# Latent attention in a two-block stack: scores from one 128-row product per head, and a new order of filler tiles

## The reference

```python
u = rms_norm(h, mix_norm[l])
c_q, c_kv, k_pe, hq, hf, hi, hg, ga, gb = split_cols(u @ w_in[l], IN_SPLITS)
y_a = mla(c_q, c_kv, k_pe, pos, q_norm[l], kv_norm[l], w_uq[l], w_ukv[l]) @ w_proj_attn[l]
y_b = hgrn2(hq, hf, hi, hg, lbs[l], hg_norm[l]) @ w_proj_rec[l]
merged = jax.nn.sigmoid(ga) * y_a + jax.nn.sigmoid(gb) * y_b
h = h + merged @ w_out[l]
# in mla: 8 heads, 64 plain + 32 rotated features
q = jnp.concatenate([q[..., :QK_NOPE], rope(q[..., QK_NOPE:], pos)], axis=-1)
k = jnp.concatenate([kv[..., :QK_NOPE], jnp.broadcast_to(k_rot, (B, L, H, QK_ROPE))], axis=-1)
s = jnp.einsum('bqhd,bkhd->bhqk', qi, k).astype(jnp.float32) * scale   # then causal softmax, times v
# rope: [x1*cos - x2*sin, x2*cos + x1*sin]
```

## Time and profile before

| | |
|---|---|
| median of 3 runs | 2515.24 us (2514.94 to 2517.25) |
| the profiled execution's own time | 2509.26 us |
| its span | 2507.3 us |
| TensorE matmul busy | 2368.4 us, 94% |
| DVE, ACT, POOL busy | 56%, 47%, 22% |
| mean granted TensorE clock over the span | 0.964 of full |
| DMA | 380 MB, mean 152 GB/s |
| chain that ended last | TensorE 64%, issue 27%, DVE 3%, POOL 2%, ACT 1% |

### The profile page before, as it was taken

The page is one execution under the profiler, slowest core; times in us unless marked ns, Lnnn a source line. Parts: engine busy times, 40 slices in busy tenths (PEclk is TensorE's granted clock), DMA queues, the critical chain, the costliest instruction groups (busy, mean ns, idle before and its releaser), DMA issues.

```text
span 2507.3 us, 50416 instructions
## 1 busy us (share of the span) xinstructions
PE 2368.4 (94%) x18374; PEld 2294.9 (92%) x18374; DVE 1412.1 (56%) x1968; ACT 1178.1 (47%) x1764; POOL 557.9 (22%) x589
## 2 busy tenths in 40 slices
PE   7999999999999999989999999986999999988998
PEld 7999886799999999877899989986999999987998
DVE  6556753455545556744655555467654655464553
ACT  5445533344435436433454355456654445445552
POOL 4321000043213310000332133123432123111320
PEclk9999998899999999988999999998999999988999
DMA  5554222245545544221355445533455455532553
GB/s 208 178 186 154 99 95 90 95 156 186 177 159 172 197 142 144 92 77 68 128 181 183 165 141 194 192 122 113 156 196 197 147 195 191 195 124 69 196 197 109
DMA packets 99270, 380.31 MB, mean 152 GB/s; under 512 B 10911, under 2 KB 13087, under 8 KB 99144
## 3 DMA queue, kind: packets, MB, share of 16 engines
q1 hardware_dynamic: 99144, 378.63, 44.5%
HBM read 377.52 MB, written 3.16 MB: 152 GB/s over the span
## 4 chain that ended last, share of the span: by engine, by line
PE 64%; issue 27%; DVE 3%; POOL 2%; ACT 1%; POOLq 1%; DVEq 1%; DMA 0%; ACTq 0%; SPq 0%
PE bank L564 20%; PE bank L566 20%; PE bank L565 20%; PE bank L625 1%; PE bank L626 1%; PE bank L627 1%; POOL midlo L1964 1%; POOLq L1919 1%; ACT whi L962 0%; PE bank L582 0%; POOLq L1907 0%; DVE cv L1694 0%; DVE wlo L1356 0%; DVE xlo L1367 0%; POOL reclo L1959 0%
## 5 line engine op out<-in xcount | busy, mean ns | idle before, releaser
L1356 DVE TENSOR_TENSOR wlo<-raw,whi 128x1024 fp32r<-128x1024 f32 (+1 forms) x660 | 873.2, 1334 | 531.6 <-ACT whi L962 530.9
L564 PE MATMUL bank<-xhi,wlo 128*128 128x272 f32 (+1 forms) x3392 | 984.2, 290 | 4.4 <-DVE z L1710 3.9
L566 PE MATMUL bank<-xhi,whi 128*128 128x272 f32 (+1 forms) x3392 | 978.0, 288 | 0.0
L565 PE MATMUL bank<-xlo,whi 128*128 128x272 f32 (+1 forms) x3392 | 976.0, 288 | 0.0
L962 ACT ACTIVATE whi<-raw 128x1024 fp32r<-128x1024 f32 (+1 forms) x660 | 729.1, 1117 | 494.1 <-PE bank L566 466.1
L564 PEld LDWEIGHTS bank<-xhi,wlo 128*128 128x128 f32 x3392 | 649.8, 192 | 7.8 <-issue 5.8
L566 PEld LDWEIGHTS bank<-xhi,whi 128*128 128x128 f32 x3392 | 648.8, 191 | 0.0
L565 PEld LDWEIGHTS bank<-xlo,whi 128*128 128x128 f32 x3392 | 648.1, 191 | 0.0
L564 PE MATMUL bank<-hidhi,wlo 128*128 128x272 f32 (+1 forms) x1408 | 400.5, 284 | 0.0
L566 PE MATMUL bank<-hidhi,whi 128*128 128x272 f32 (+1 forms) x1408 | 399.5, 284 | 0.0
L565 PE MATMUL bank<-hidlo,whi 128*128 128x272 f32 (+1 forms) x1408 | 399.3, 284 | 0.0
(11 more groups left out here) (319 smaller groups left out, 2662.0 us busy)
## 6 DMA issues: line engine op xcount, KB each, us to landing
raw<-ffn_gu SPq DMA_DIRECT2D x352, 512.0 KB, 3.5
raw<-ffn_down SPq DMA_DIRECT2D x128, 704.0 KB, 4.1
raw<-mix SPq DMA_DIRECT2D x120, 512.0 KB, 3.5
raw<-rec SPq DMA_DIRECT2D x28, 512.0 KB, 3.7
raw<-kv SPq DMA_DIRECT2D x16, 512.0 KB, 4.0
raw<-att SPq DMA_DIRECT2D x16, 512.0 KB, 3.8
bias_rows<-rows SPq DMA_DIRECT2D x8, 256.0 KB, 4.3
bias<-bias_rows SPq DMA_DIRECT2D x1, 1536.0 KB, 8.0
```

The source lines that it names most:

```text
L564: pe.matmul(out, wlo[:, slot, w], xh(i), start=(i == 0), stop=False)
L565: pe.matmul(out, whi[:, slot, w], xl(i), start=False, stop=False)
L566: mm = pe.matmul(out, whi[:, slot, w], xh(i), start=False, stop=(i == last))
L1356: dve.tensor_tensor(wlo[:, k, 0:cols], raw[:, k, 0:cols], whi[:, k, 0:cols].bitcast(F32), ALU.subtract).then_inc(lo_made, 1)
```

## The change

Each head gets one 128-row query `qh` and key `kh`: for even heads 64 plain rows, then 32 rotary rows and 32 rotary rows with halves swapped; for odd heads the other way about. The query's rows are multiplied by one factor (`rq`) that holds scale, norm and 1, cos or sin; the key's swapped rows repeat the rotated key, so that the sum over 128 rows is the whole score. So `query_key` is one product, DVE's rotation of the queries goes, `uq` 6 and 7 are evicted like the others, and `kn`'s eviction becomes two half-height ones. `krot` is copied into the eight keys by ACT (`key_turn`). The constants grow by 2x272 columns.

In the order, `hgate` 1 to 3 now stand ahead of level 0, and the tiles behind the levels are `cq` to `gb` 3. `gb` 4 to 6 fill between rec_out and the norms. Around the first head stand `gb` 7, `pr` 0, 1 and `ga` 0; the heads' fillers come from a table `HEAD_FILL`, one `ga`, two `pr` or (once) two `ga` each. `norm` of head h+1 stands ahead of the filler of head h; `tail_norm` is a step of its own, right behind the tail's scores and apart from the transposes (`tail`), and `pair_lo` is a step ahead of filler as well.

```diff
+    tiles += run("cq", 0, 3) + run("ckv", 0, 2) + run("kpe", 0, 2) + run("gb", 0, 7)
+    tiles += run("uq", 0, 8) + run("ukv", 0, 8) + run("gb", 7, 8) + run("pr", 0, 2) + run("ga", 0, 1)
+    return tiles + [tile for fill in HEAD_FILL for tile in fill] + run("pa", 0, 8) + run("out", 0, 8)
+HEAD_FILL = ([("ga", 1)], [("pr", 2), ("pr", 3)], [("ga", 2)], [("ga", 3), ("ga", 4)], [("pr", 4), ("pr", 5)],
+             [("ga", 5)], [("pr", 6), ("pr", 7)], [("ga", 6)], [("ga", 7)])
...
+    plain = np.ones((NOPE, T), np.float32)
+    turned = np.concatenate([np.tile(np.cos(ang), (2, 1)), -np.sin(ang), np.sin(ang)])
+    put("turn", np.concatenate([np.concatenate([plain, turned]), np.concatenate([turned, plain])], 1))
...
+    steps += [tile("hgate", m) for m in range(1, 4)]
     for level in range(LEVELS + 1):
...
-        steps.append(("tile", HGATE + 1 + level))
+        steps.append(("tile", CQ + level))
...
+    steps += [("tail_norm", 0), ("norm", 0), tile("pr", 0), tile("pr", 1), ("tail", 0), tile("ga", 0)]
     for h in range(HEADS):
-        steps.append(("norm", h))
         if h + 1 < HEADS:
             steps.append(("scores", h + 1))
         if h == 2:
             steps.append(("tail_scores", 1))
         steps.append(("turn", h))
-        steps += [("tile", next(fill)), ("tile", next(fill))]
+        if h + 1 < HEADS:
+            steps.append(("norm", h + 1))
+        if h == 2:
+            steps.append(("tail_norm", 1))
+        if h % 2 == 0 and h >= 2:
+            steps.append(("pair", h // 2 - 1))
+        steps += [tile(*at) for at in HEAD_FILL[h]]
         if h == 3:
             steps.append(("tail", 1))
         steps.append(("attend", h))
+    steps += [("pair", 3)] + [tile(*at) for at in HEAD_FILL[HEADS]]
...
-                r, r2 = NOPE * (hd % 2), ROPE * (hd % 4)
-                pe.matmul(out, qn[r:r + NOPE, hd // 2, at_t:at_t + size], kn[r:r + NOPE, hd // 2, 0:keys],
-                          start=True, stop=False)
-                return pe.matmul(out, qr[r2:r2 + ROPE, hd // 4, at_t:at_t + size], krot[r2:r2 + ROPE, 0:keys],
-                                 start=False, stop=True)
+                return pe.matmul(out, qh[:, hd, at_t:at_t + size], kh[:, hd, 0:keys], start=True, stop=True)
...
+                    elif step == "key_turn":
+                        act.wait_ge(krot_made, l + 1)
+                        for r, first in ((NOPE, 0), (0, 1)):
+                            turned = krot[r:r + 2 * ROPE, :].unsqueeze(1).to_broadcast([2 * ROPE, HEADS // 2, T])
+                            last = act.activation(kh[r:r + 2 * ROPE, first::2, :], turned, ACT.Copy)
+                        last.then_inc(keys_turned, 1)
...
-                        dve.scalar_tensor_tensor(to, b, QK_SCALE, rlat[:, 0, :], ALU.mult, ALU.mult
-                                                 ).then_inc(tile_read, 1)
-                        if m >= 6:
...
+                        dve.tensor_tensor(qh[:, m, :], b, rq[:, m % 2, :], ALU.mult).then_inc(tile_read, 1)
+                    elif kind == "ukv" and m < 4:
+                        dve.tensor_tensor(kh[0:NOPE, 2 * m, :], b[0:NOPE], rlat[0:NOPE, :], ALU.mult)
+                        dve.tensor_tensor(kh[NOPE:P, 2 * m + 1, :], b[NOPE:P], rlat[NOPE:P, :], ALU.mult).then_inc(tile_read, 1)
...
+                    elif step == "latent_back" and i == 0:
+                        dve.wait_ge(lat_back, l * 2 + 1)
+                        back = bank[NORM][:, BACK:BACK + T].unsqueeze(1).to_broadcast([P, 2, T])
+                        dve.scalar_tensor_tensor(rq[:, :, :], const("turn", 2 * T).rearrange("p (two t) -> p two t", two=2),
+                                                 QK_SCALE, back, ALU.mult, ALU.mult).then_inc(lat_rstd, 1)
```

More of the change, by code:

```diff
@@ L65 @@
 HI, HGATE, CQ, CKV, KPE, KPS = (AT[tile] for tile in (("hi", 0), ("hgate", 0), ("cq", 0), ("ckv", 0), ("kpe", 0), ("kpe", 1)))
-UQ, UKV, G2, PA, OUT = (AT[tile] for tile in (("uq", 0), ("ukv", 0), ("gb", 4), ("pa", 0), ("out", 0)))
+UQ, UKV, G2, PA, OUT = (AT[tile] for tile in (("uq", 0), ("ukv", 0), ("gb", 7), ("pa", 0), ("out", 0)))
 PARTS = {"uq": 3, "ukv": 2, "pr": 4, "pa": 4}
@@ L93 @@
 _at = 0
-for _name, _n in (("ones", P), ("mean", P), ("ident", P), ("cos", T), ("sin", T), ("causal", 3 * P),
+for _name, _n in (("ones", P), ("mean", P), ("ident", P), ("cos", T), ("sin", T), ("turn", 2 * T), ("causal", 3 * P),
                   ("causal_tail", T), ("eps", 1)):
@@ L172, in mixer_order @@
             steps.append(("take", level - 1))
-        steps.append(("tile", HGATE + 1 + level))
[L174 to L179, removed]
+        steps.append(("tile", CQ + level))
+    steps += [("rec_out", 0), ("rec_out", 1), tile("gb", 4), ("rec_out", 2), ("rec_out", 3), ("key_turn", 0), tile("gb", 5),
+              ("sums", 0), tile("gb", 6), ("latent_back", 0), ("rec_norm", 0), tile("uq", 0), tile("uq", 1),
+              ("latent_back", 1), ("rec_norm", 1), tile("uq", 2), tile("uq", 3), ("rec_norm", 2), tile("uq", 4),
+              tile("uq", 5), ("rec_norm", 3)]
+    steps += [("tile", t) for t in range(UQ + 6, G2)] + [("turn_v2", 0), tile("gb", 7), ("scores", 0), ("tail_scores", 0)]
+    steps += [("tail_norm", 0), ("norm", 0), tile("pr", 0), tile("pr", 1), ("tail", 0), tile("ga", 0)]
     for h in range(HEADS):
-        steps.append(("norm", h))
         if h + 1 < HEADS:
@@ L236, in z_before @@
     last, before = {}, {}
-    for t in [*range(HI), *range(HGATE, UQ), UQ + 6, UQ + 7, *range(UKV + 4, G2 + 4), *(AT["ga", m] for m in range(KD))]:
+    for t in [*range(HI), *range(HGATE, UQ), *range(UKV + 4, G2 + 1), *(AT["ga", m] for m in range(KD))]:
         before[t] = last.get(z_place(t))
@@ L1135, in mixer @@
                         root.then_inc(mix_std, 1)
-                    elif step == "latent_back":
-                        act.wait_ge(lat_back, l * 2 + i + 1)
-                        act.activation(rlat[:, i, :], bank[NORM][:, BACK:BACK + T], ACT.Copy).then_inc(lat_rstd, 1)
+                    elif step == "key_turn":
[4 more added lines that the diff above has]
+                        last.then_inc(keys_turned, 1)
+                    elif step == "latent_back" and i == 1:
+                        act.wait_ge(lat_back, l * 2 + 2)
+                        act.activation(rlat[:, :], bank[NORM][:, BACK:BACK + T], ACT.Copy).then_inc(lat_rstd, 1)
                     elif step == "rec_norm" and i >= 1:
@@ L1587, in tail_scores, with tail_norm @@
                     dve.tensor_reduce(negmax[:, g, 2:3], sct[:, g, :], AX_X, ALU.max, negate=True).then_inc(tail_max, 1)
-                def tail(g):
+                def tail_norm(g):
                     dve.wait_ge(tail_exp, l * 2 + g + 1)
@@ L1603, in normalize @@
                     last.then_inc(probs_normed, 1)
-                    if hd % 2 == 0 and hd >= 2:
-                        pair_lo(hd // 2 - 1)
                 def pair_lo(pair):
@@ L2047, in mixer_weights @@
     nope, rope = q[:, :, :NOPE], q[:, :, NOPE:]
-    uq = np.concatenate([t.reshape(Q_LORA, -1) for t in (nope, rope, rope[:, :, swap])], 1)
+    turned = np.concatenate([rope, rope[:, :, swap]], 2)
+    heads = [(nope, turned)[::-1 if h % 2 else 1] for h in range(HEADS)]
+    uq = np.concatenate([part[:, h] for h, parts in enumerate(heads) for part in parts], 1)
     kv = w_ukv.reshape(KV_LORA, HEADS, NOPE + V_HEAD)
```

40 lines of the change are left out of this document (17 added, 23 removed).

## The result

Before: 2515.09 us, median of 4 runs (2508.56 to 2517.25). After: 2424.39 us, median of 4 runs (2421.50 to 2425.70). The ratio is 0.965, with a 95% interval of 0.9636 to 0.9665: 88 us less by the ratio, 90.7 by the medians. The forecast was 2425.8.

The account below looks back on a forecast made before the run. TensorE, busy 94% of the span, was taken as the bound. Terms A to F sum to 89.4 us, from the profiled 2509.3 to 2419.9, or 2425.8 us for a median; 2410 to 2440 had 0.72, the range reached 2455.

Parts of the forecast that it names:

- A: Heads' scores: one 128-row product per size instead of alternating 64 and 32 rows, 2.08 to 0.65 us per head; 22.9 us saved.
- B: Heads' tails: one product of 0.46 us instead of two of 0.57, for 16 heads; 10.9 us saved.
- C: TensorE's clock in the heads: most of the 32 us lost to 1.2 GHz comes back; 26 us saved, bounds 0 and 32.
- D: TensorE's waits in the heads: 9.6 us per layer go, a new one of 0.9 appears; 17.4 us saved net.
- E: Levels: gates moved out shorten the first wait from 2.8 to 1.5 us, half clock shrinks; 9.6 us saved, bounds 0 and 23.
- F: uq and ukv: two DVE rotations go, four half-height evictions come; 2.6 us saved, between 0 and 3.8.
- The new wait: First head: DVE, held by gb 7, finishes its chain at 6.2 us, TensorE needs the bank at 5.3; 0.9 us.
- Exposed loads of 128 rows: Rival: weight loads of the new score and tail products stay exposed; 11.4 us back, 2437 us; chance 0.05.
- The clock not coming back: Rival: sparse work keeps the clock low, so C and 7 us of E are lost; 2459 us; chance 0.12.
- The head's chain coming to light: Rival: with one filler per head the chain grows from 3.1 to 5.4 us; 32 us back, 2458 us; chance 0.08.
- The slower outcome: Rival: TensorE sits at 1.2 GHz through levels and heads; slower if beyond 89 of 250 us; chance 0.03.

Follow-up runs that it names:

- experiment 2: Two kernels: changed kernel with each score product split in two, alternating 64 and 32 rows (2471.3 us) or both of the same 64 rows (2428.97 us).
- experiment 1: The change's two parts, each alone: new products with the old order (2451.81 us), and new order with the old products (2474.45 us).
- products_alone: Changed kernel with the tile order, gates and normalising of the kernel before, keeping the 128-row products: 2451.81 us, ratio to before 0.9758.
- experiment 4: Kernel before with one edit: each group's four 64-row tail products together, then the four of 32 rows, instead of alternating: 2482.23 us, ratio 0.9888.
- tails_one_place: Changed kernel with all four tail products of a group written into the same 32 output rows: 2422.39 us, one execution.
- tails_twice_aabb: Changed kernel with each of a group's four tail products issued twice in a row into the same 32 output rows: 2424.77 us, one execution.
- experiment 5: Changed kernel with the three gate tiles back between the levels and gb 0 to 2 in their place ahead of level 0: 2425.05 us, ratio 0.9647.
- norms_behind: Changed kernel with the normalisings behind the filler tiles, as in the kernel before: 2467.44 us, ratio 0.9825.
- order_alone: Kernel before with the new order of tiles and steps, keeping its 64- and 32-row products: 2474.45 us, ratio 0.9851.
- rows_64_same: Changed kernel with each score product replaced by two of the same 64 rows: 2428.97 us, ratio 0.9667.

## Why the prediction was right, and where its steps were not

The sum was 89.4 us, the changed stretches gave 90.1, the medians 90.7. By terms, for both layers:

| term | forecast | measured | from |
|---|---|---|---|
| A scores | 22.9 | 21.4 | 2.08 to 0.74 us, 16 heads |
| B tails, at full clock | 10.9 | 15.8 | 8 x 0.57 to 0.60 us, 4 groups |
| C clock in the heads | 26 | 28.1 | the 32 of the earlier trace rows less 0.03 x 62.2 in each layer |
| D waits in the heads | 17.4 | 13.8 | 9.6 to 2.7 us per layer |
| E levels | 9.6 | 11.0 | 4.9 and 6.1 |
| F uq, ukv | 2.6 | 2.1 | 1.1 and 1.0 |

The terms A to D sum to 79.1 where the heads gained 77.1; the rest is overlap in this way of dividing them.

That the sum came so close is partly luck. B was 4.9 us too small and D 3.6 too large, A was 1.5 too large and C 2.1 too small, and these errors largely cancel. The starting point has a scatter of its own too: the kernel before, measured again beside the experiments, had medians of 2508.8 to 2510.9 us, 4 to 6 below the one that the forecast started from.

**A and C.** Right in size and in cause: alternating 64 and 32 rows costs beyond the columns (experiment 2), and the clock follows it (experiment 1). The waits of 2.9 us, named as a second cause, are one, but the smaller: with them the heads of products_alone lose 5.1 us to half clock in layer 0, without them 1.9. What the prediction did not see is that the tails' products, and not the scores, brought most of the rest (experiment 4).

**B.** The step that failed is "One of 272 columns at 128 rows: 0.46 us" *times sixteen*. The price is right for one (0.49 in tails_one_place), but four in four places take 0.60 us together.

**D.** The new wait was forecast at 0.9 us ahead of `ga` 0; there are 1.3 ahead of the tail's transposes, 0.5 ahead of `ga` 0 and 0.9 for `pt`. The first follows from B: the tails took 0.60 us where I counted 1.84, so TensorE reached the transposes 1.24 us earlier, while DVE's chain took 5.9 us as forecast (6.2). tails_twice_aabb shows it: 0.48 us more of tails, 0.8 instead of 1.3 us of wait. The wait for `pt` I missed altogether: on ACT the second head's exponentials stand ahead of the copy, and wait for a mask that DVE makes behind `ga` 0's weight split.

**E.** The size is right, the reason for the first wait is not. "Without the gates between, one of them is out of its chain: 2.8 to 1.5" was the step; the wait fell to 1.2, and it did so with gates between as well (experiment 5). The three tiles ahead of level 0 did that, be they gates or `gb`. Taking the gates and their table loads out of the levels is worth 5 us of the 11.

**Rivals.** Exposed loads of 128 rows: refuted, 0.74 us per head. The clock not coming back: 0.97 in the heads, 1.00 in the levels. The head's chain coming to light: not in this order, but norms_behind shows that it was near, at 43 us. The middle stretch (`rec_out` to the first scores) stays at 0.90, as before. The slower outcome did not come.

## What to carry to other kernels

When short products alternate in the number of rows they use, look at what one costs from start to start: put all of one height together, or stack the operands to full height; here sixteen reordered products per layer were worth 28 us. Products with few output rows belong side by side in different places of a bank. And when a stage gets faster, ask what arrives too early: filler that covered a chain with 1.2 us to spare covers it no more when 1.2 us of work is gone.

## What the runs showed of the hardware

Not expected: with alternating heights products of 272 columns and 32 output rows stood 0.57 us apart, one after the other, at full clock; with one height four took 0.60 us together; and pairs into the same place did not hold up their neighbours (eight in 1.08 us).

In one stretch, more work took less time. tails_twice_aabb issues four more products per group than the changed kernel, and its heads take 61.20 us instead of 62.20 in each layer. The whole is not faster (2424.77 us): in layer 0 the stretch ahead of the heads took 52.69 us at a clock of 0.87, against 51.07 at 0.90, though nothing was changed there. The longer tails shorten the wait ahead of the transposes from 1.3 to 0.8 us, and `ga` 0 behind it stays at full clock: 3.1 us (393.58 to 396.71) where the changed kernel has 4.64. The profile shows the two together; that the shorter wait is what kept the clock is likely, and rows_64_same and tails_one_place, with no wait ahead of the transposes at all, stand at 1.00 in the heads too; but no run isolates it.

Half clock also came without any wait: in order_alone, in the heads, TensorE waits for nothing and stands at 0.88.
